# Picks made head by head between the query weights, and scaled one-hot tables made by VectorE alone

## What is computed

```python
qr = (hb @ w_pq).reshape(b, t, 8, 2, 128)                  # queries, 8 heads with 2 halves
sc = einsum('bthpd,hpnd->bthpn', qr, sub_keys)             # 128 scores in each half
s_top, i_top = top_k(sc, 16)
cand = s_top[..., 0, :, None] + s_top[..., 1, None, :]     # 16 x 16 sums
c_top, c_pos = top_k(cand.reshape(b, t, 8, 256), 16)
expert = i0 * 128 + i1                                     # 8 x 16 = 128 picks for each token
g = softmax(c_top)
a = gelu(einsum('bthkd,btd->bthk', u_tab[expert], hb))
out = einsum('bthk,bthkd->btd', g * a, v_tab[expert])
```

## Time and profile before

| what | value |
|---|---|
| median of 3 runs | 1708.07 us (1706.79 to 1709.87) |
| the profiled execution | 1710.41 us, its span 1708.4 us |
| TensorE busy | 1667.7 us, 98% of the span |
| VectorE busy | 1022.4 us, 60% |
| ScalarE busy | 404.7 us, 24% |
| GpSimd busy | 247.3 us, 14% |
| memory traffic | 569.77 MB, mean 334 GB/s |

### The profile page before, as it was taken

One profiled execution on the slowest core, in us unless ns is written; L12 is line 12 of the kernel. 1 busy time (PEld: TensorE's weight loads), 2 busy tenths in 40 slices (PEclk: granted clock), 3 DMA queues, 4 the chain that ended last, 5 costly groups with the idle time before them and its releaser, 6 DMA issues.

```text
span 1708.4 us, 28369 instructions
## 1 busy us (share of the span) xinstructions
PE 1667.7 (98%) x11296; PEld 1585.1 (93%) x11296; DVE 1022.4 (60%) x1688; ACT 404.7 (24%) x1019; POOL 247.3 (14%) x250
## 2 busy tenths in 40 slices
PE   7999999999999999999999999999989999999999
PEld 5768888887999999999999999999989999999998
DVE  5426695765547999767777777736435334443444
ACT  6547567646542000022112111200000000000000
POOL 1020000000001031222212112203113111111110
PEclk9999999999999999999999999999999999999999
DMA  9664446466556699899999999999999999999997
GB/s 337 231 146 133 138 127 195 146 224 222 168 177 234 238 367 410 348 421 421 422 422 422 422 422 422 422 402 381 422 412 421 422 422 422 422 421 422 422 421 295
DMA packets 106373, 569.77 MB, mean 334 GB/s; under 512 B 11088, under 2 KB 13264, under 8 KB 47376
## 3 DMA queue, kind: packets, MB, share of 16 engines
q1 hardware_dynamic: 56480, 216.51, 34.5%
q0 software_dynamic: 31696, 220.50, 32.0%
q10 hardware_dynamic: 18144, 132.13, 18.9%
HBM read 563.04 MB, written 4.46 MB: 332 GB/s over the span
## 4 chain that ended last, share of the span: by engine, by line
PE 62%; DMA 22%; DVE 12%; issue 3%; ACT 1%; POOL 0%; SPq 0%; DVEq 0%; ACTq 0%
PE ps L1472 32%; DMA late<-in_u_rows,sel 18%; PE ps L1219 5%; PE ps L1221 5%; PE ps L1220 5%; PE ps L1417 4%; PE ps L1238 2%; PE ps L1375 2%; PE ps L1374 2%; PE ps L1373 2%; DVE late L1081 2%; DMA raw<-in_w_in 1%; DMA raw<-in_v_tab 1%; DVE w_lo L778 1%; DVE acts L1057 1%
## 5 line engine op out<-in xcount | busy, mean ns | idle before, releaser
L1085 DVE SCALAR_TENSOR_TENSOR acts<-late,sel,acts 128x2048 f32<-128x2048 f32 x77 | 181.1, 2351 | 246.9 <-DMA late<-in_v_tab,sel 246.0
L1472 PE MATMUL ps<-acts,raw 128*128 (+1 forms) x2048 | 285.3, 300 | 6.6 <-DMA raw<-in_v_tab 6.6
L1417 PE MATMUL ps<-acts,late 128*128 128x160 f32 x2048 | 288.4, 300 | 0.0
L1472 PEld LDWEIGHTS ps<-acts,raw 128*128 128x128 f32 x2048 | 281.7, 191 | 6.8 <-issue 6.8
L1417 PE MATMUL ps<-acts,raw 128*128 128x160 f32 x2048 | 286.6, 299 | 0.0
L1472 PE MATMUL ps<-acts,late 128*128 (+1 forms) x2048 | 284.2, 299 | 0.0
L778 DVE TENSOR_TENSOR w_lo<-raw,w_hi 128x512 fp32r<-128x512 f32 (+1 forms) x288 | 188.9, 682 | 159.0 <-ACT w_hi L518 158.1
L1417 PEld LDWEIGHTS ps<-acts,late 128*128 128x128 f32 x2048 | 282.2, 191 | 0.0
L1417 PEld LDWEIGHTS ps<-acts,raw 128*128 128x128 f32 x2048 | 280.5, 190 | 0.0
L1472 PEld LDWEIGHTS ps<-acts,late 128*128 128x128 f32 x2048 | 280.1, 190 | 0.1
L1081 DVE SCALAR_TENSOR_TENSOR late<-late,acts 128x2048 f32<-128x2048 f32 x76 | 173.8, 2290 | 79.3 <-DMA late<-in_u_rows,sel 79.0
(11 more groups left out here) (208 smaller groups left out, 1494.3 us busy)
## 6 DMA issues: line engine op xcount, KB each, us to landing
raw<-in_w_in SPq DMA_DIRECT2D x72, 512.0 KB, 3.7
raw<-in_u_tab SPq DMA_DIRECT2D x33, 1024.0 KB, 9.3
late<-in_u_tab SPq DMA_DIRECT2D x33, 1024.0 KB, 9.3
raw<-in_v_tab SPq DMA_DIRECT2D x32, 1024.0 KB, 10.0
raw<-in_v_tab ACTq DMA_DIRECT2D x32, 1024.0 KB, 10.0
late<-in_v_tab SPq DMA_DIRECT2D x32, 1024.0 KB, 10.0
late<-in_v_tab ACTq DMA_DIRECT2D x32, 1024.0 KB, 10.0
raw<-in_u_tab ACTq DMA_DIRECT2D x31, 1024.0 KB, 9.5
```

The source lines that it names most:

```text
L1085: V.scalar_tensor_tensor(acc, row[n % NROW], w_sp[:, n - N_OWN:n - N_OWN + 1], acc, ALU.mult, ALU.add).then_inc(row_used, 1)
L1417: ins = mm(ps[:, q, 0:N_DN], ring[q][:, k * P:k * P + P], hF[:, k, :], start=k == 0, stop=k == KD - 1)
L1472: ins = mm(ps[:, pair_bank(k // 2), at:at + N_DN], ring[q][:, k * P:k * P + P], acts[:, ds(i * (4 * N_DN) + q * N_DN, N_DN)], start=first ...
```

## The change

**Picks.** The query weights come head by head, in the order 6, 7, 0, 1, 2, 3, 4, 5 (`HEAD_ORDER`; the host reorders `w_pq` and `sub_keys`). TensorE makes a head's scores as soon as its two query columns are there, between two units of weights. VectorE runs the first three heads of the sparse tile (`N_AHEAD` = 3) step by step between the query weights' `split_lo` halves, one half after each step. The rest follows after the weights: 5 heads with two rows behind each, then the 8 heads of the other tile with two rows behind each, then six rows. Row numbers are made head by head, the copy to the helpers too (`lend_picks`): POOL issues it and waits for it ahead of the gathers 0, 16, 32, 48, 64 and 80. The picks' scratch moves out of the activations' region, so one MEMSET (2560 columns, which waited for `slotT_mm`) goes, and the first grows from 6144 to 8704 columns.

**Tables.** `hots` makes `hot1` as before, and `hot0` with one VectorE instruction for each of the four tokens, compare and multiply in one. `hot_scale` on ScalarE goes.

**End of the U stage.** The GELU of the sparse dot products moves from V chunk 3 to U chunk 120, what VectorE does with it to chunk 122, and five rows of `v_tab` are summed in the last chunks of the U stage. 32 + 4 rows of `u_tab` are then done before chunk 52 instead of 18 + 4, so row 96 comes at chunk 111 instead of 125.

```diff
+        HEAD_ORDER = [(h + 6) % NH for h in range(NH)]
+        N_AHEAD = 3
...
             def gather(n):
+                if n == 0:
+                    pool.wait_ge(hs_ready, 2)
+                if n == 1:
+                    pool.wait_ge(piece_used, 2 * B_U)
...
+            def lend_picks(h):
+                pool.wait_ge(idx_ready, N_AHEAD + h)
+                at = N_OWN + TOPK * (h % 2)
+                pool.dma_start(idx[helpers, TOPK * h:TOPK * h + TOPK], idx[lenders[h // 2], at:at + TOPK]).then_inc(idx_in, 16)
+                pool.wait_ge(idx_in, 16 * (h + 1))
+
+            def gathers(first, end):
+                for n in range(first, end):
+                    if n < N_OWN and n % TOPK == 0:
+                        lend_picks(n // TOPK)
+                    gather(n)
...
+            for hp in range(N_AHEAD):
+                top_k(0, hp, weights_low)
+                row_numbers(hp)
+                weights_low()
+                weights_low()
...
+            for hp in range(N_AHEAD, NH):
+                top_k(0, hp)
+                row_numbers(hp)
+                next_row(2)
+            for hp in range(NH):
+                top_k(1, hp)
+                next_row(2)
             next_row(6)
...
-                for f, dst in ((1, hot1), (0, hot0)):
-                    ins = V.tensor_tensor(dst, iota[:, :].unsqueeze(1).to_broadcast([P, 4, P]),
-                                          slotT[:, f, 4 * g:4 * g + 4].unsqueeze(2).to_broadcast([P, 4, P]), ALU.is_equal)
-                ins.then_inc(hot_eq, 1)
+                V.tensor_tensor(hot1, iota[:, :].unsqueeze(1).to_broadcast([P, 4, P]),
+                                slotT[:, 1, 4 * g:4 * g + 4].unsqueeze(2).to_broadcast([P, 4, P]), ALU.is_equal)
+                for k in range(4):
+                    t = 4 * g + k
+                    ins = V.tensor_scalar(hot0[:, k, :], iota[:, :], slotT[:, 0, t:t + 1], slotT[:, 2, t:t + 1], ALU.is_equal, ALU.mult)
+                ins.then_inc(hot_done, 1)
...
+                if c == NKEY - 6:
+                    assert rows_done[0] == N_OWN
+                    dve.wait_ge(a_done, 1)
...
+                if c > NKEY - 6:
+                    next_row()
...
+            def head_scores(hp):
+                pe.wait_ge(qr_done, 2 * hp + 2)
...
+            for c in range(16):
...
+                    wide_piece(c // 2, B_PQ, 4 * (c % 2) + j, c % 2)
...
+                if c >= 2 and c % 2 == 0:
+                    head_scores(c // 2 - 1)
+            head_scores(NH - 1)
```

More of the change, by code:

```diff
@@ L494, in _ @@
                 pool.dma_start(lent[lenders[i], :], acc_copy[helpers, :]).then_inc(lent_in, 16)
-                for n in range(N_OWN + (i + 1) * N_TURN + NROW - 1, min(N_OWN + (i + 2) * N_TURN + NROW - 1, 2 * N_OWN)):
-                    gather(n)
+                gathers(N_OWN + (i + 1) * N_TURN + NROW - 1, min(N_OWN + (i + 2) * N_TURN + NROW - 1, 2 * N_OWN))
             pool.wait_ge(row_used, 2 * N_OWN)
@@ L724, in gelu @@
                 nc.scalar.activation(dst, ps[:, c % 4, 0:N_DN], ACT.Gelu).then_inc(gelu_done, 1)
-            def hot_scale(g):
-                act.wait_ge(hot_eq, g + 1)
-                for k in range(4):
-                    nc.scalar.activation(hot0[:, k, :], hot0[:, k, :], ACT.Copy, scale=slotT[:, 2, 4 * g + k:4 * g + k + 1]).then_inc(hot_done, 1)
-            scale_after = {group_chunk(g) - 1: g for g in range(N_GRP)}
             def odd_unit(c):
@@ L1023, in _ @@
                                     ALU.add).then_inc(hF_done, 1)
-            with dve.Fori(1, U_PQ // 4) as i:
-                for j in range(4):
-                    split_lo(i * 4 + (B_PQ + j), j)
-            dve.wait_ge(gain_row_in, 16)
-            for i in range(2):
-                V.scalar_tensor_tensor(hs[i], x2[0], rs_x[:, 0:1], row[0], ALU.mult, ALU.mult).then_inc(hs_ready, 1)
-            V.tensor_reduce(help_count, ident[:, helpers], AX, ALU.add).then_inc(mask_set, 1)
-            dve.wait_ge(mask_set, 1)
-            V.tensor_scalar(own_row, help_count, -1.0, 1.0, ALU.mult, ALU.add).then_inc(mask_set, 1)
+            for u in range(4, 8):
+                split_lo(B_PQ + u, u)
             steps = [0]
@@ L1376, in wide_piece @@
                 ins.then_inc(piece_used, 1)
-            def wide_pair(i, base, out_done, before=lambda piece: None):
-                for c in range(2):
-                    if not (isinstance(i, int) and i == 0):
-                        pe.wait_ge(out_done, i * 2 + (c - 1))
-                    for j in range(4):
-                        before(4 * c + j)
-                        wide_piece(i, base, 4 * c + j, c)
             def rest_of_norm(piece):
@@ L1529 @@
     columns = lambda g: g.reshape(-1, 128).T
+    by_head = [(c + 12) % 16 for c in range(16)]
     sent = {
```

201 lines of the change are left out of this document (106 added, 95 removed).

## The result

| | before | after |
|---|---|---|
| median | 1706.89 us (20 runs, 1706.30 to 1710.87) | 1710.82 us (20 runs, 1706.78 to 1714.21) |
| profiled execution | 1710.41 us, span 1708.4 us | 1710.99 us, span 1709.2 us |

The ratio is 1.0023, with a 95% interval of 1.0017 to 1.0029. The change makes the kernel 0.23% slower. The forecast was 1702.7 us and faster. One execution of the study, of the kernel with both mends, ran in a slower state of the chip (1722.46 us at a granted clock of 0.948) and is left out.

What follows compares the result with a forecast made beforehand. TensorE, busy 98%, and memory at 421 to 422 GB/s were both taken as near their limit. 1710.41 + 0.6 - 6.0 - 4.0 + 4.0 = 1705.0 us, less 2.34 us for the profiled execution: 1702.7 us, 8-in-10 range 1694 to 1711.

Steps and rivals of the forecast that it cites:

- Last head's scores: Ahead of the U stage: the last head's scores now wait for ScalarE's copy of the last column, +0.6 us.
- Picks between the weights: Query weights: VectorE's selection steps between the halves cost TensorE 0, up to 3 us if wrong.
- First gate: First gate product in U: earlier rows take away TensorE's wait and the low clock behind it, -6.0 us.
- Tables: Gates in U: VectorE making both tables without ScalarE shifts TensorE once, -1.1 us.
- The rule weighed ahead: Each second table would wait up to 0.98 us for a GpSimd row request, 1.0 us more in the sum; not followed.
- Fewer pairs at memory's pace: Later gates of U: 22 pairs 0.41 us over TensorE's pace, 9.1 us instead of 12.0, -2.9 us.
- Copies of row numbers: POOL's queue in U: waits for the copies ahead of rows 48, 64 and 80, taken as +4.0 us.
- the two bounds: Cost of the row-number copies: 0 if memory makes up for the gaps, 14.7 us for three at 4.9 us each.
- V, 0: V stage: same loads in the same order, so the 8.6 us lost behind the `x_rest` load stay.
- Rival A: Row-number copies stall the gates, three gaps of 4.9 us passed on in full: +10.7 us, 1713.4 us; 15%.
- The longer pairs that were to show the copies: Sign in the U stage: three longer pairs near gates 8, 16 and 24, where rows 48, 64 and 80 stand.
- Rival B: Gates run free, memory never setting the pace: all 12.0 us of the later gates go, 1690.7 us; 12%.

Runs made afterwards that it cites:

- both mends: Changed kernel with the row-number copies asked for eight requests ahead and `x_rest` loaded on GpSimd's queue; 1695.06 us, ratio 0.9939.
- `x_rest` late: Changed kernel with the `x_rest` load moved on SP's queue from behind V unit 31 to behind V unit 119; 1707.21 us, ratio 1.0007.
- the copies ahead: Changed kernel with the same six row-number copies, each asked for eight row requests ahead of its wait; 1705.76 us, ratio 0.9992.
- The pair with the added products: Kernel with copies asked for ahead, plus 23 unused TensorE products in front of gate 1 (1706.00 us) or of gate 37 (1711.61 us).
- one copy: Changed kernel with the row numbers of heads 1 to 5 copied in one go ahead of gather 16; 1705.87 us, ratio 0.9995.
- one copy and the old tables: Changed kernel with heads 1 to 5 copied at once and tables made as before (VectorE compares, ScalarE scales); 1707.17 us, ratio 0.9998.
- copies of 8: Changed kernel with a row-number copy and its wait ahead of every eighth gather instead of every sixteenth; 1718.63 us, ratio 1.0079.
- the second profile of before: The kernel before, unchanged, profiled once more: 1707.51 us, span 1705.6 us; median 1707.54 us, ratio 1.0000.
- the load on GpSimd's queue: `x_rest` load moved from SyncE's to GpSimd's queue: in the changed kernel with one copy 1696.13 us, in the kernel before 1708.12 us.

## Why the prediction was wrong

**Last head's scores, +0.6 us: right.** TensorE waits 0.47 us for ScalarE's copy (row 521.05 of after). In the start of U it can't be seen, which varies by more.

**Picks between the weights, 0: right.** TensorE has no wait for `w_lo` in the query weights. The larger MEMSET blocks a step of VectorE, as in the earlier trace rows. VectorE and GpSimd of after:

```profile
529.04 6.20 DVE L1069 TENSOR_SCALAR acts<-acts 128x16 f32<-128x16 f32 x1
...
527.84 7.37 POOL L485 MEMSET acts<- 128x8704 f32 x1
```

Both end at 535.2 us, and it cost nothing.

**First gate, -6.0 us: the step that failed.** The place itself was read rightly. In after, which has copies with their waits in front of it, 3.5 us were won at gate 1 (in the same kernel with `x_rest` late, none). With the copies ahead it was 6.0 us, of 7.1 that the terms of the first gate and the tables make. What failed is the next step, by which this went into the sum. The prediction had said that memory sets the pace of the later gates, and then added the first gate's gain to that stage as if it didn't. A stop of TensorE lets the rows get ahead, and the pairs behind it go faster. Of the 6.0 us, 1.1 are left at gate 31 (524.68 for 525.78 us), hardly more than the up to 1.0 us by which two profiles of one kernel differ. The pair with the added products shows the same from the other side: 6.25 us put in at gate 1 cost 0.2 us.

**Tables, -1.1 us: wrong.** The four scaled tables took 1.11 us and not 0.9 (row 830.20), so VectorE needs 1.7 us for a group (829.59 to 831.31) and not 1.5; the chain before took 2.6. At gate 1 the new tables brought 4.0 us in the changed kernel with one copy, and cost 1.6 us in the kernel before. Neither is left at gate 31, for the same reason as above. The line of L1133 in after gives its steps, in ns:

```profile
L1133 DVE TENSOR_SCALAR early<-iota,slotT x160: 330/343/437, 744.7 to 1126.0; 128x128 f32<-128x128 f32 x160
```

None of the 160 took over 437 ns. The four from 785.03 us run beside a row request of GpSimd from 784.78 to 785.92 us, and take 1.11 us like the four from 795.27 us, which have no request beside them. The rule weighed ahead, of the Trainium skill ("SBUF — State Buffer", Who interferes with whom), would hold some of them back for up to a whole request, 0.94 to 1.14 us here. This trace doesn't show that.

**Fewer pairs at memory's pace, -2.9 us: nearly right.** From gate 31 to V the changed kernel takes 81.9 us for 83.9: -2.0 us. The last row of U stands in front of gate 32 in it, in front of gate 39 before, and the pairs behind it come at 9.59 us. It isn't shown to be the rows' alone: with one copy and the old tables, whose rows end as early, the same stretch takes 86.0 us, with a stop of 2.01 us at gate 32.

**Copies of row numbers, +4.0 us: too small.** They cost 5.95 us (612.57 for 606.62 us to V), and 5.1 us of the median. The cost lies between the two bounds, and what it rests on held: what is lost is close to the time without a transfer. The size was wrong, since the prediction counted only the copies ahead of rows 48, 64 and 80. Those ahead of rows 16 and 32 are waited for too, 14.85 and 14.94 us. Gate 1 comes 2.5 us later in after than with the copies ahead, and each of the three later waits left memory idle for 2.4 us.

**V, 0: wrong by 2.0 us.** TensorE's part of V is 570.2 to 570.7 us in five versions of the changed kernel with its new tables, 569.3 with copies of 8, 569.8 with the old tables, and 568.5 to 568.7 us in three of before. Stop and low clock together are 10.25 us in after (7.47, and 11.64 for 8.86), and 8.25 us in the second profile of before (5.30, and 11.81 for 8.86). The 2.0 us belong to the stop behind `x_rest`: with the load on GpSimd's queue both take 560.4 us within 0.1. Why the stop is longer in the changed kernel was not settled.

**The sum.** From the first product of U on, the prediction had -6.0 - 4.0 + 4.0 + 0 = -6.0 us, the first -4.0 being the tables and the fewer pairs. Measured against before's second profile: -3.1 for the first gate, the tables and the fewer pairs together, +5.95 for the copies, +2.0 in V, 4.9 us in all. So of the 10.9 us of error 6.0 come from the first gate and the tables, whose gain is made at gate 1 and gone at gate 31, 0.9 from the fewer pairs, 2.0 from the size of the copies, and 2.0 from V. That the time fell inside the range for 8 in 10 is luck: the range was wide, and it was not reached by the mechanism that was to give it.

Of the rivals, none was it. Rival A had the right sign for the right reason, but put the 10.7 us of its copies on top of the same -6.0. The longer pairs that were to show the copies were found at gates 9 and 25, and none at gate 17: with 19.21 us the wait there was the shortest of the three. The kernel with `x_rest` late, which is the same up to V, shows the same from the other side. There the waits are 19.23, 22.00 and 18.92 us, and the only stop of the three is at gate 17:

```profile
895.32 2.23 POOL L463 DMA_INDIRECT late<-in_u_rows,sel  x1 [22.00 <-DMA sel<-sel]
```

```profile
912.45 2.08 PE L1464 MATMUL ps<-early 128*128 128x128 f32 x8 [4.17 <-DVE early L1133]
```

So in these two traces a wait of 21.9 us or more gave a stop, and one of 19.2 us or less none. Rival B's 1690.7 us took off all 12.0 us where the forecast already had 2.9 of them; added on rightly it is 1693.6 us. Nothing came of it: memory went on setting the pace.

## What to carry to other kernels

Where memory sets the pace of a stage, keep one account of bytes for the whole stage. A stop inside it costs little more than the time in which memory stands still too, and so a stop that is taken away brings little more than that. A small copy that waits in a queue behind large ones cost nothing here once it was asked for eight requests ahead of its wait; ask early. When an edit moves time on an engine that ends close to another one, try it together with the edit that frees the other: here the one alone cost 4 us or, with its waits mended, gave about 1 us, which is not clear of the noise; the other alone gave nothing, and both together over 11 us.

## What was not expected of the hardware

A copy of 16 columns for 32 partitions lands 2.1 us after its request on an empty GpSimd queue, and 17.4 us after it in the median of all six, 22.8 us at most, when it has rows ahead of it in the queue. And the 1.31 MB of `x_rest` in SyncE's queue stop TensorE for 4.73 to 7.92 us, with a granted clock of 0.76 over the next 12 us in after, though they are 3.1 us of memory's time at 422 GB/s; in GpSimd's queue the first part of it lands 23.0 us after its request, and TensorE doesn't stop.
